# A hybrid decoder layer on one core: x scaled ahead of its turning, and turned by transposes

## The chip, the cores and the metric
The kernel runs on one core of a Trainium2 chip. The metric is the device time in microseconds of one launch. The kernel before took 1552.87 us as the median of three runs (1552.44 to 1555.18).

## What is computed
One layer over 512 tokens and 16 meta tokens in front (528 rows, 2048 features, float32), cut here to what the change touches:

```
h    = concat([meta_tokens, x])                               # 528 x 2048
hn   = h * rsqrt(mean(h * h, axis=-1) + 1e-6) * pre_norm_w    # one factor a token, one a feature
proj = hn @ w_in                                              # 2048 x 8320 columns
# two groups of heads work on proj (RWKV-7 time mixing, differential attention),
# each is multiplied by a SiLU gate
y    = concat([y_r, y_d]) @ w_out
out  = (h + rms_norm(y, post_norm_w))[16:]
```

## The kernel before
The core's five engines each have a program of their own, and semaphores tie them together: SP (SyncE) issues the loads, ScalarE, VectorE and GpSimd (POOL) do elementwise work, TensorE multiplies and turns.

All projections need hn with features on partitions: 16 feature tiles of 128 partitions by 528 tokens. Products are made in three parts to keep float32 precision: each operand is split in a high and a low part (`hn_hi`, `hn_lo`, `w_hi`, `w_lo`), and three products are summed (`feature_tile`, L517). The weights come in units of four 128x128 tiles through a ring of four slots `w_raw`; ScalarE casts the high part (`split_hi`, L843) and POOL makes the low part (`split_lo`, L1086), which frees the slot for SP's next load.

At the start x comes in with tokens on partitions: four tiles `xin[:, t, :]` of 128 x 2048 and the 16 meta rows `xm`. SP loads meta, x tile 0, the constants c32 (they hold the identity), x tiles 1 to 3, ten small parameter rows and then four weight units. The factor of a token goes through three engines, in the order meta, 0, 1, 2, 3: ScalarE squares a tile and sums it (L852), VectorE makes mean + eps (L1150), POOL raises it to -1/2 (L1094). VectorE then multiplies the identity by the factors of each tile (`norm_d`, L1156), copies the turned parameters (`par`, L1159) and makes six small derived ones.

TensorE first turns the parameters (L524), waits for `par_made` and for all five `norm_spread`, and enters the loop that this case is about (L530 to L548). In step k it turns feature tile k by five float32 products, x's tile as the stationary operand and the scaled diagonal as the moving one: 16 meta columns (L535) and four times 128 (L539), into `ma` for even k and `mb` for odd k. From k = 2 on it waits for `hn_lo_made` of k-2, since the PSUM tensor has to be free. ScalarE makes `hn_hi` from it with pre_norm_w as scale (L857), and VectorE `hn_lo` (L1170). From k = 4 on step k also makes the six products L517 of feature tile k-4 for the low-rank tile. ScalarE casts one weight unit in each of the steps 0 to 3.

Behind the loop TensorE goes on with the last four feature tiles and the projections of the first head pair. VectorE sums up the lambda products, clears the padded buffers and signals `zeroed`; then the low-rank tile is finished, and the loops over head pairs follow.

Of the kernel before, what the change touches and what calls it, by code (L numbers as in the profile page):

```python
# [34 lines left out]
P = 128  # L35
D = 2048
# [35 lines left out]
for _name, _rows in (("mu_r", 8), ("mu_k", 8), ("mu_v", 8), ("mu_l", 1), ("w0", 8), ("a0", 8), ("k_k", 8), ("k_a", 8),  # L72
                     ("r_k", 8), ("gn_w", 8), ("gn_b", 8), ("pre", 16), ("sub", 1)):
    PC[_name] = _n
    _n += _rows
N_PAR = _n


# [39 lines left out]
def hybrid_layer(nc, x, meta_tokens, pre_norm_w, w_in, rwkv_mu, rwkv_w0, rwkv_w_up, rwkv_a0, rwkv_a_up,  # L118
# [3 lines left out]
    with ctx:  # L122
# [110 lines left out]
        junk = carve("start", "junk", D)  # L233
        norm_d = carve("start", "norm_d", 5 * P)

# [47 lines left out]
        def s(name):  # L283
            if name not in S:
                S[name] = sem(name)
            return S[name]
# [132 lines left out]
        def _(sp):  # L419
            xs = x[0].rearrange("(t p) d -> p t d", p=P)  # L420
            sp.dma_start(xm[0:META, :], meta_tokens).then_inc(s("meta_in"), 16)
            sp.dma_start(xin[:, 0, :], xs[:, 0, :]).then_inc(s("x_in0"), 16)
            sp.dma_start(c32[:], c32_dram).then_inc(s("const_in"), 16)
            for t in range(1, 4):
                sp.dma_start(xin[:, t, :], xs[:, t, :]).then_inc(s(f"x_in{t}"), 16)
            sp.dma_start(par_rows[0:25, :], rwkv_mu[0].rearrange("(r c) -> r c", c=P)).then_inc(s("par_in"), 16)
# [77 lines left out]
        def _(pe):  # L504
# [21 lines left out]
            pe.wait_ge(s("par_made"), 1)  # L526
            pe.wait_ge(s("norm_spread"), 5)


            for k in range(KT + LORA_LAG):  # L530
                if k < KT:
                    o = (ma, mb)[k % 2]
                    if k >= 2:
                        pe.wait_ge(s("hn_lo_made"), k - 1)
                    mm(o[:, TURN:TURN + META], xm[0:META, k * P:(k + 1) * P], norm_d[0:META, 4 * P:4 * P + META],  # L535
                       start=True, stop=True)
                    for t in range(4):
                        at = TURN + META + t * P
                        last = mm(o[:, at:at + P], xin[:, t, k * P:(k + 1) * P], norm_d[:, t * P:(t + 1) * P],  # L539
                                  start=True, stop=True)  # L540
                    last.then_inc(s("x_turned"), 1)
                if k >= LORA_LAG:
                    h, c = divmod(k - LORA_LAG, UK)
                    pe.wait_ge(s("hn_lo_made"), k - LORA_LAG + 1)
                    pe.wait_ge(s("lo_done"), h + 1)
                    last = feature_tile(tiles[0], h, h, c, True)
                    if c == UK - 1:
                        last.then_inc(s("unit_used"), 1)  # L548
# [286 lines left out]
        def _(act):  # L835
# [9 lines left out]

            for n, t in enumerate((4, 0, 1, 2, 3)):
                act.wait_ge(s(f"x_in{t}" if t < 4 else "meta_in"), 16)
# [233 lines left out]
        def _(pool):  # L1081
# [8 lines left out]
            pool.wait_ge(s("power_made"), 1)  # L1090
            for n, t in enumerate((4, 0, 1, 2, 3)):
                rows = P if t < 4 else META
# [48 lines left out]
        def _(dve):  # L1141
# [4 lines left out]

            for n, t in enumerate((4, 0, 1, 2, 3)):
                rows = P if t < 4 else META
                dve.wait_ge(s("norm_sq"), n + 1)
                TS(norm_s[0:rows, 5 + t:6 + t], norm_s[0:rows, t:t + 1], 1.0 / D, EPS, ALU.mult,  # L1150
                   ALU.add).then_inc(s("norm_var"), 1)
            dve.wait_ge(s("const_in"), 16)
            for n, t in enumerate((4, 0, 1, 2, 3)):
                rows = P if t < 4 else META
                dve.wait_ge(s("norm_pow"), n + 1)
                TS(norm_d[0:rows, t * P:t * P + rows], ident[0:rows, 0:rows], norm_s[0:rows, 10 + t:11 + t], None,  # L1156
                   ALU.mult).then_inc(s("norm_spread"), 1)
            dve.wait_ge(s("par_turned"), 1)
# [316 lines left out]
```

## Time and profile before
| what | value |
|---|---|
| median of the runs | 1552.87 us |
| span of the profiled execution | 1549.4 us |
| PE, PE weight loads busy | 93%, 81% of the span |
| DVE, ACT, POOL busy | 50%, 37%, 31% |
| share of the chain that ended last | PE 76%, DVE 14% |
| mean granted TensorE clock | 0.983 |

The span runs from the first to the last instruction of one profiled execution; of that execution the page gives no other time. PE is TensorE, DVE VectorE, ACT ScalarE. L535 is line 535 of the kernel. The granted clock is given as a share of 2.4 GHz.

### The profile page before, as it was taken

How to read it: one execution, taken by the hardware profiler on the slowest of the kernel's cores; microseconds unless marked ns; L12 is line 12 of the kernel's file. 1: busy time of each engine (PE TensorE's matmuls, PEld its weight loads, DVE VectorE, ACT ScalarE, POOL GpSimd, SP SyncE). 2: the span in 40 equal slices, each digit the busy share in tenths (PEclk: the TensorE clock that was granted, in tenths of full speed). 3: DMA queues.
4: the chain of work that ended last, by engine and by line, in shares of the span. 5: the costliest groups of instructions: out<-in, count | busy, mean ns of one | idle time of the engine just before them, and what ended most of it. 6: DMA issues, size and time to landing. Idle time of an engine off the chain costs nothing.

```text
span 1549.4 us, 26552 instructions
## 1 busy us (share of the span) xinstructions
PE 1436.7 (93%) x9929; PEld 1257.3 (81%) x9929; DVE 767.5 (50%) x1560; ACT 576.3 (37%) x1204; POOL 476.7 (31%) x361
## 2 busy tenths in 40 slices
PE   5998999999999999999999988999999999989994
PEld 4988889788897888988879786978878879768883
DVE  2326566665666666667666544344343443540003
ACT  5332343333434334343333253434444434432321
POOL 2341232222322223232232232334333333324442
PEclk9999999999999999999999999999999999999997
DMA  5221111111111111111111121222222222215322
GB/s 190 71 84 42 42 44 49 50 41 41 42 47 44 43 44 42 47 42 41 47 42 49 50 73 50 70 69 70 69 68 68 61 68 68 68 58 205 117 95 111
DMA packets 151637, 101.43 MB, mean 65 GB/s; under 512 B 6446, under 2 KB 140688, under 8 KB 150416
## 3 DMA queue, kind: packets, MB, share of 16 engines
q1 hardware_dynamic: 151584, 100.71, 21.2%
q8 instruction: 35, 0.57, 0.1%
q14 instruction: 18, 0.15, 0.0%
HBM read 96.49 MB, written 4.19 MB: 65 GB/s over the span
## 4 chain that ended last, share of the span: by engine, by line
PE 76%; DVE 14%; issue 4%; ACT 3%; DMA 1%; POOL 1%; DVEq 0%; SPq 0%; ACTq 0%; POOLq 0%
PE tile L517 39%; PE ma L623 3%; PE tile L784 2%; PE tile L785 2%; PE tile L786 2%; PE ma L644 1%; PE ma L658 1%; DVE arena L1333 1%; PE ma L651 1%; PE mb L709 1%; PE ma L661 1%; DVE arena L1308 1%; PE mb L765 1%; PE ma L786 1%; PE ma L784 1%
## 5 line engine op out<-in xcount | busy, mean ns | idle before, releaser
L1086 POOL TENSOR_TENSOR w_lo<-w_raw,w_hi 128x512 fp32r<-128x512 f32 x324 | 429.3, 1326 | 1012.7 <-ACT w_hi L843 1012.6
L517 PE MATMUL tile<-hn_hi,w_hi 128*128 128x264 f32 (+1 forms) x1696 | 455.5, 331 | 0.0
L517 PE MATMUL tile<-hn_hi,w_lo 128*128 128x264 f32 (+1 forms) x1696 | 436.6, 320 | 0.0
L517 PE MATMUL tile<-hn_lo,w_hi 128*128 128x264 f32 (+1 forms) x1696 | 435.7, 320 | 0.0
L843 ACT CAST w_hi<-w_raw 128x512 fp32r<-128x512 f32 x324 | 200.3, 619 | 425.3 <-PE tile L517 315.1
L517 PEld LDWEIGHTS tile<-hn_hi,w_hi 128*128 128x128 f32 x1696 | 280.0, 190 | 25.6 <-issue 7.2
L517 PEld LDWEIGHTS tile<-hn_hi,w_lo 128*128 128x128 f32 x1696 | 277.6, 190 | 13.3
L517 PEld LDWEIGHTS tile<-hn_lo,w_hi 128*128 128x128 f32 x1696 | 277.3, 190 | 11.0 <-issue 0.5
L1321 DVE TENSOR_TENSOR arena<-ma,c 128x384 f16<-128x384 f32 x120 | 66.7, 556 | 54.7 <-PE ma L644 52.5
L979 ACT ACTIVATE arena<-ma 128x384 f16<-128x384 f32 x120 | 58.5, 487 | 89.0 <-PE ma L658 88.5
L1330 DVE CAST arena<-ma 128x384 f16<-128x384 f32 x120 | 66.6, 555 | 49.3 <-PE ma L661 47.9
L623 PE MATMUL ma<-arena 128*128 128x192 f32 x288 | 59.6, 343 | 12.2 <-issue 12.2
L1405 DVE COPY arena<-mb 128x128 f32<-128x128 f32 x32 | 9.3, 290 | 103.6 <-PE mb L767 103.6
L976 ACT ACTIVATE arena<-ma 128x384 f32<-128x384 f32 x72 | 35.2, 489 | 68.2 <-PE ma L651 68.2
L623 PEld LDWEIGHTS ma<-arena 128*128 128x128 f32 x288 | 47.8, 195 | 15.3 <-issue 13.9
L784 PE MATMUL tile<-w_hi,hn_hi 128*128 128x512 f32 x128 | 53.6, 419 | 5.5 <-DVE hn_lo L1423 5.5
L1308 DVE TENSOR_TENSOR arena<-arena,c 128x384 f16<-128x384 f16 x144 | 52.2, 404 | 0.8
L785 PE MATMUL tile<-w_lo,hn_hi 128*128 128x512 f32 x128 | 51.6, 403 | 0.0
L786 PE MATMUL tile<-w_hi,hn_lo 128*128 128x512 f32 x128 | 51.3, 401 | 0.0
L1101 POOL TENSOR_TENSOR arena<-arena,power 128x4 f32<-128x4 f32 (+2 forms) x25 | 39.1, 1566 | 33.1 <-DVE arena L1409 13.3
L992 ACT ACTIVATE arena<-arena 128x128 f32<-128x128 f32 x72 | 28.8, 400 | 52.7 <-DVE arena L1354 36.5
L658 PE MATMUL ma<-arena 128*128 128x128 f16 x360 | 41.3, 223 | 3.8 <-DVE arena L1321 3.8
(252 smaller groups left out, 2242.5 us busy)
## 6 DMA issues: line engine op xcount, KB each, us to landing
w_raw<-w_in SPq DMA_DIRECT2D x260, 256.0 KB, 2.8
w_raw<-w_out SPq DMA_DIRECT2D x64, 256.0 KB, 2.5
big<-x SPq DMA_DIRECT2D x4, 1024.0 KB, 8.9
arena<-x SPq DMA_DIRECT2D x4, 1024.0 KB, 9.7
out<-big SPq DMA_DIRECT2D x4, 768.0 KB, 3.6
arena<-post_norm_w SPq DMA_DIRECT2D x1, 1024.0 KB, 4.9
out<-big SPq DMA_DIRECT2D x4, 256.0 KB, 2.5
arena<-table_rope SPq DMA_DIRECT2D x2, 264.0 KB, 2.9
```

The source lines that it names most:

```text
L517: last = mm(o[:, at:at + n], w[:, slot, cols], t[:, kt, tok:tok + n], start=(kt == 0 and w is w_hi and t is hn_hi), stop=(kt == KT - 1 and ...
L623: last = mm(ma[:, c * 256:c * 256 + P + CH], pad[:, cs[c], :], apad_r[:, cs[c], :], start=True, stop=True)
L658: last = mm(bank(0, c), bl(xt16, c), bl(z16, c), start=True, stop=True)
L784: mm(banks[t], hn_hi[:, k, y], w_hi[:, k % RING, :], start=(k == 0), stop=False)
L785: mm(banks[t], hn_hi[:, k, y], w_lo[:, k % RING, :], start=False, stop=False)
L786: last = mm(banks[t], hn_lo[:, k, y], w_hi[:, k % RING, :], start=False, stop=(k == KT - 1))
L843: nc.scalar.copy(w_hi[:, slot, :], w_raw[:, slot, :]).then_inc(s("hi_done"), 1)
L979: A(x16, ma[:, 0:W], ACT.Copy).then_inc(s("x_taken"), 1)
L1086: T(w_lo[:, slot, :], w_raw[:, slot, :], w_hi[:, slot, :].bitcast(F32), ALU.subtract).then_inc(s("lo_done"), 1)
L1308: level = lambda l, o: TT(o, g3(ab_hi), level_masks[:, l, :].unsqueeze(1).broadcast_to([P, GC, P]), ALU.mult)
L1321: TT(g3(z16), g3(ma[:, 512:512 + W]), ident16.unsqueeze(1).broadcast_to([P, GC, P]), ALU.add).then_inc(s("zz_taken"), 1)
L1330: V.tensor_copy(xt16, ma[:, 512:512 + W]).then_inc(s("xt_taken"), 1)
```

## The change
The diagonals `norm_d` go. VectorE multiplies each tile of x, and the meta rows, by its tokens' factors in place, over all 2048 columns (`scaled`), and TensorE turns the scaled tiles with `nc.tensor.transpose` and the plain identity. The squares of tiles 1 and 3 are taken on VectorE (`squares_here`), those of meta, 0 and 2 stay on ScalarE. TensorE waits for `x_scaled` of all five, and for the parameters as before. SP loads x's four tiles ahead of the constants.

```diff
-        norm_d = carve("start", "norm_d", 5 * P)
+        junk_d = carve("start", "junk_d", D)
...
-            sp.dma_start(xin[:, 0, :], xs[:, 0, :]).then_inc(s("x_in0"), 16)
+            for t in range(4):
+                sp.dma_start(xin[:, t, :], xs[:, t, :]).then_inc(s(f"x_in{t}"), 16)
             sp.dma_start(c32[:], c32_dram).then_inc(s("const_in"), 16)
-            for t in range(1, 4):
-                sp.dma_start(xin[:, t, :], xs[:, t, :]).then_inc(s(f"x_in{t}"), 16)
...
-            pe.wait_ge(s("norm_spread"), 5)
+            pe.wait_ge(s("x_scaled"), 5)
...
-                    mm(o[:, TURN:TURN + META], xm[0:META, k * P:(k + 1) * P], norm_d[0:META, 4 * P:4 * P + META],
-                       start=True, stop=True)
+                    nc.tensor.transpose(o[:, TURN:TURN + META], xm[0:META, k * P:(k + 1) * P],
+                                        ident[0:META, 0:META])
                     for t in range(4):
                         at = TURN + META + t * P
-                        last = mm(o[:, at:at + P], xin[:, t, k * P:(k + 1) * P], norm_d[:, t * P:(t + 1) * P],
-                                  start=True, stop=True)
+                        last = nc.tensor.transpose(o[:, at:at + P], xin[:, t, k * P:(k + 1) * P], ident)
...
-            for n, t in enumerate((4, 0, 1, 2, 3)):
+            for n, t in enumerate((4, 0, 2)):
                 act.wait_ge(s(f"x_in{t}" if t < 4 else "meta_in"), 16)
...
+            def variance(t):
+                rows = P if t < 4 else META
                 TS(norm_s[0:rows, 5 + t:6 + t], norm_s[0:rows, t:t + 1], 1.0 / D, EPS, ALU.mult,
                    ALU.add).then_inc(s("norm_var"), 1)
+            def squares_here(t):
+                dve.wait_ge(s(f"x_in{t}"), 16)
+                if t == 3:
+                    dve.wait_ge(s("norm_sq_dve"), 1)
+                STT(junk_d, token_rows(t), 1.0, token_rows(t), ALU.mult, ALU.mult,
+                    accum_out=norm_s[:, t:t + 1]).then_inc(s("norm_sq_dve"), 1)
+            def scaled(n, t):
+                rows = P if t < 4 else META
                 dve.wait_ge(s("norm_pow"), n + 1)
-                TS(norm_d[0:rows, t * P:t * P + rows], ident[0:rows, 0:rows], norm_s[0:rows, 10 + t:11 + t], None,
-                   ALU.mult).then_inc(s("norm_spread"), 1)
+                v = token_rows(t)
+                TS(v, v, norm_s[0:rows, 10 + t:11 + t], None, ALU.mult).then_inc(s("x_scaled"), 1)
+            dve.wait_ge(s("norm_sq"), 1)
+            variance(4)
+            dve.wait_ge(s("norm_sq"), 2)
+            variance(0)
+            scaled(0, 4)
+            scaled(1, 0)
+            squares_here(1)
+            dve.wait_ge(s("norm_sq_dve"), 1)
+            variance(1)
+            dve.wait_ge(s("norm_sq"), 3)
+            variance(2)
+            scaled(2, 1)
+            squares_here(3)
+            dve.wait_ge(s("norm_sq_dve"), 2)
+            variance(3)
+            scaled(3, 2)
+            scaled(4, 3)
+            dve.wait_ge(s("const_in"), 16)
             dve.wait_ge(s("par_turned"), 1)
```

## Rows read from the trace of the kernel before
**Rows 1.** Head of the page.
```profile
span 1549.4 us, 26552 instructions
```
**Rows 2.** Chain of waits, first 90 us: start us, us, what.
```profile
15.21 2.01 ACT arena L852 x2
...
17.33 1.07 DVE arena L1156 x5
...
18.62 0.60 PE ma L535 x2
...
26.86 1.09 PE ma L539 x8
27.95 0.72 PE tile L517 x6
28.67 0.32 PE mb L535 x2
28.99 1.09 PE mb L539 x8
30.08 0.73 PE tile L517 x6
...
51.48 38.53 PE tile L517 x315
```
**Rows 3.** Turning: groups by shape (count, busy us, mean ns), and timeline near 108 us.
```profile
L539 PE MATMUL ma<-arena,big 128*128 128x128 f32 x64 | 10.2, 307 | 0.0
L597 PE MATMUL mb<-c,arena 128*128 128x128 f32 x40 | 5.9, 279 | 1.0
108.19 0.74 PE L597 MATMUL mb<-c,arena 128*128 128x128 f32 x5
```
**Rows 4.** Timeline, 19 to 28 us: start us, us, instruction.
```profile
19.16 2.08 PE L539 MATMUL ma<-arena,big 128*128 128x128 f32 x8
...
25.38 1.16 PE L539 MATMUL mb<-arena,big 128*128 128x128 f32 x8
...
26.57 0.70 ACT L857 ACTIVATE hn_hi<-mb,par 128x528 fp32r<-128x528 f32 x1 [0.46 <-PE mb L539]
...
27.17 0.61 ACT L843 CAST w_hi<-w_raw 128x512 fp32r<-128x512 f32 x1
27.31 0.77 DVE L1170 SCALAR_TENSOR_TENSOR hn_lo<-mb,par,hn_hi 128x528 fp32r<-128x528 f32 x1 [0.90 <-ACT hn_hi L857]
```
**Rows 5.** Timeline, 52 to 55 us.
```profile
52.94 0.21 DVE L1175 TENSOR_TENSOR arena<-arena 128x64 f32<-128x64 f32 x1
53.00 1.30 POOL L1086 TENSOR_TENSOR w_lo<-w_raw,w_hi 128x512 fp32r<-128x512 f32 x1 [1.06 <-ACT w_hi L843]
...
53.44 0.94 DVE L1175 TENSOR_TENSOR arena<-arena 128x64 f32<-128x64 f32 x1
```
**Rows 6.** VectorE's groups by shape: count, busy us, mean ns, idle before.
```profile
L1374 DVE TENSOR_TENSOR arena<-arena 128x512 f32<-128x512 f32 x8 | 11.0, 1375 | 0.7 <-ACT arena L880 0.7
...
L1267 DVE SCALAR_TENSOR_TENSOR arena<-arena 128x576 f32<-128x576 f32 x8 | 6.0, 751 | 0.0
...
L1372 DVE TENSOR_TENSOR arena<-xk,arena 128x512 f32<-128x512 f32 x8 | 5.5, 685 | 0.0
...
L1400 DVE TENSOR_SCALAR arena<-arena 128x528 f32<-128x528 f32 x8 | 4.0, 496 | 0.3
...
L1400 DVE TENSOR_SCALAR arena<-arena 128x144 f32<-128x144 f32 x8 | 2.4, 295 | 0.3
```
**Rows 7.** Timeline of the start.
```profile
8.91 0.57 POOL L1094 TENSOR_TENSOR arena<-arena,power 128x1 f32<-128x1 f32 x1 [2.51 <-DVE arena L1150]
10.03 1.91 ACT L852 ACTIVATE arena<-big 128x2048 f32<-128x2048 f32 x1 [1.39 <-DMA big<-x]
...
16.54 0.40 PE L524 MATMUL ma<-c,arena 98*128 98x98 f32 x1 [16.54 <-DMA arena<-diff_subln_w]
```
**Rows 8.** Windows: stretch, length, busy us of PE, PEld, DVE, ACT, POOL, granted clock, DMA.
```profile
120.00:125.00 5.00, 4.87 (x17) 4.90 (x18) 2.06 (x5) 0.00 (x0) 0.00 (x0) 0.50 0.00 0
125.00:130.00 5.00, 4.57 (x40) 4.14 (x40) 2.74 (x7) 2.14 (x5) 1.28 (x1) 0.96 0.04 10
...
900.00:904.00 4.00, 2.24 (x19) 2.03 (x17) 3.90 (x6) 2.40 (x5) 1.31 (x1) 1.00 0.24 68
```

More of the change, by code:

```diff
@@ L76 @@
 N_PAR = _n
+NORM_ORDER = (4, 0, 1, 2, 3)
 def constants():
@@ L1090, in _ @@
             pool.wait_ge(s("power_made"), 1)
-            for n, t in enumerate((4, 0, 1, 2, 3)):
+            for n, t in enumerate(NORM_ORDER):
                 rows = P if t < 4 else META
@@ L1144, in _, with token_rows @@
             TT, STT, TS = V.tensor_tensor, V.scalar_tensor_tensor, V.tensor_scalar
-            for n, t in enumerate((4, 0, 1, 2, 3)):
+            def token_rows(t):
+                return xin[:, t, :] if t < 4 else xm[0:META, :]
+            def variance(t):
                 rows = P if t < 4 else META
-                dve.wait_ge(s("norm_sq"), n + 1)
                 TS(norm_s[0:rows, 5 + t:6 + t], norm_s[0:rows, t:t + 1], 1.0 / D, EPS, ALU.mult,
                    ALU.add).then_inc(s("norm_var"), 1)
-            dve.wait_ge(s("const_in"), 16)
-            for n, t in enumerate((4, 0, 1, 2, 3)):
+            def squares_here(t):
[5 more added lines that the diff above has]
+            def scaled(n, t):
                 rows = P if t < 4 else META
                 dve.wait_ge(s("norm_pow"), n + 1)
-                TS(norm_d[0:rows, t * P:t * P + rows], ident[0:rows, 0:rows], norm_s[0:rows, 10 + t:11 + t], None,
-                   ALU.mult).then_inc(s("norm_spread"), 1)
+                v = token_rows(t)
[18 more added lines that the diff above has]
+            dve.wait_ge(s("const_in"), 16)
             dve.wait_ge(s("par_turned"), 1)
```

## The prediction
> **What bounds the kernel now.** I read the page's header first: the span is 1549.4 us [rows 1]. It is 3.5 us under the median of the runs, 1552.87, and the page gives no other time for that execution. I work on the span and carry the difference over to the median. Next I read the chain of waits over the first 90 us [rows 2]. It has three parts. Until 18.6 us no product of the layer runs: the chain goes over the loads of x, two squares on ScalarE and five small VectorE multiplications, and TensorE starts at 18.62. From there to 51.5 us the chain never leaves TensorE for long: it alternates between turning one feature tile of x (L535 for the 16 meta rows, L539 for the other 512) and the six low-rank products of an earlier tile (L517). From 51.5 it stays in L517 for 38.53 us. So a microsecond off the turning loop is a microsecond for everything behind it, and a microsecond of later start costs one.
>
> The turning is matrix products with a scaled diagonal. The view by shapes shows 64 records at L539 for each of the two PSUM tensors, 128 for 16 x 4 = 64 products: two records for each f32 product [rows 3]. The turns that the kernel makes elsewhere as real transposes have 40 records at L597 for 8 x 5 transposes, one each [rows 3]. Five of them lie in 0.74 us, of which the last takes 0.27: (0.74 - 0.27) / 4 = 0.12 us apart [rows 3]. In the loop one L539 record costs 1.09 / 8 = 0.136 us on the chain [rows 2].
>
> **The change part by part.** (1) *Turning by transposes.* A turn now costs 0.32 + 1.09 = 1.41 us [rows 2] and has ten records; it keeps five. Half is 0.70; with 0.12 apart it would be 0.6. I take 0.70, because the meta piece and the change of PSUM bank keep their edges. A step of the loop is then 0.70 + 0.73 (six L517) = 1.43 instead of 2.14 us. Is another engine next? ScalarE needs 0.70 for hn_hi, VectorE 0.77 for hn_lo [rows 4], and turn k+2 has to wait for hn_lo of k: 0.70 + 0.70 + 0.77 + about 0.12 of handing over = 2.3 us per two steps, against 2.86 on TensorE. So TensorE still sets the pace, with 0.28 us a step to spare. From turn 5 to turn 15 there are eleven such turns: 11 x 0.71 = **7.8 us gained**.
>
> (2) *The first five turns.* TensorE is slow there: the first eight records take 2.08 us, 0.25 each, those from 25.38 on 1.16 us, 0.14 each [rows 4]. The granted clock in the profile says 1.00 for this stretch too, so I go by the spacing: the lower of the two levels, 1.2 GHz, until some 4.8 us after the first product. Before, turn 4 ends and the first L517 starts 27.95 - 18.62 = 9.33 us after TensorE's start [rows 2]. After, with T as the start, turns 0 and 1 end at T+1.27 and T+2.54. hn_lo of 0 is ready at T+2.8, so turn 2 runs to T+4.1. ScalarE has a weight cast of 0.61 us [rows 4] between its hn_hi, so hn_lo of 1 is ready at T+4.1 and turn 3 ends at T+5.4. hn_lo of 2 comes at T+5.6, and turn 4 (at full clock by then) ends at T+6.4. **2.9 us gained**, not the 4.6 that the halved records would give, since here the hn_hi-hn_lo loop is next. POOL's first w_lo (1.30 us each [rows 5]) is ready at about T+4 and isn't late.
>
> (3) *The start.* The five diagonal multiplications (1.07 us [rows 2]) and two of ScalarE's squares go; VectorE gets two squares over 2048 columns and five scalings over 2048 in place, all in one queue, and TensorE waits for the last. Durations: the scaling by a pointer scalar, in place, in SBUF (L1400), takes 295 ns for 144 columns and 496 for 528 [rows 6]: 0.52 ns a column, for 2048 columns 496 + 1520 x 0.52 = 1.29 us. That row is the same operation in the same place, so it decides; the upper bound is one column in 1.03 ns as below, 2.27 us. The square is a two-input operation: 685 ns for 512 and 751 for 576 columns [rows 6], 1.03 ns each, so 751 + 1472 x 1.03 = 2.27 us; upper bound by L1374, 1375 ns for 512, twice that. Reading the accumulator is taken as 0.15. Nothing excludes a little less than any of these, by 0.1 each.
>
> Now the queue. VectorE is free at 8.85, when POOL takes the power for x's first tile [rows 7]; the meta power is long done. Two scalings: 11.4. Square of tile 1, which landed before 10.03 even in the old order [rows 7]: 13.85. Two variances: 14.15. POOL's power, 0.57 with handing over 0.65 [rows 7]: 14.8. Scaling of 1: 16.1. Square of 3: 18.5. Variance 18.7. Scalings of 2 and 3: 21.3. Copy of the parameters, the 0.22 us between 18.40 and 18.62 in the chain [rows 2]: 21.6. There is a second effect. VectorE's two-input operation of 64 columns took 0.21 us alone and 0.94 beside POOL's w_lo, ending with it [rows 5]. POOL's powers of 0.57 fall beside VectorE's new long operations three times, so each may wait for the other: 0 to 1.7 us. I take 0.5: T = 22.1, **3.5 us lost** against 18.62. Bounds: 21.0 to 23.3 with the durations above, 33 with both upper bounds.
>
> (4) *Order of the loads.* x's tiles 1 to 3 go ahead of the 368 KB of constants in SP's queue; ten small parameter loads stay behind both. The bytes in front of the parameters are the same, so their turn at 16.54 [rows 7] stays, far ahead of the new T. Tile 3 may come 0.9 us earlier; VectorE reaches it at 16.1, so it is worth nothing: VectorE hides it. Nothing else on SP moves. The constants aren't needed before that 16.54. The loss if this cover fails is at most about 1 us.
>
> (5) *What lies behind.* The rest of the start on VectorE (lambda, clearing, the signal that lets ScalarE finish the low-rank tile) is counted from hn_lo of tile 15, the weight loads from POOL's w_lo: all move with the loop. TensorE never waits between 51.5 and 90 us [rows 2], so I let the whole shift through to the end.
>
> Sum: + 3.5 - 2.9 - 7.8 = -7.2 us. 1552.87 - 7.2 = **1545.6 us**.
>
> **Rivals.** *A late clock.* What raises the clock might be products, and not transposes. Then the low level lasts past the first products: turn 4 costs 1.27, and a step costs 1.27 + 2 x 0.73 = 2.7 us until the clock rises. If it rises 4.8 us after the first L517 as it did after the first product, two steps and a half run slow: 2.5 x 1.3 = 3.2 us. Time: 1548.8. For it: the four turns before the first L517 will hold no product at all, and no row shows the clock rise on transposes alone. Against: nothing in the trace tells the two apart. The Trainium skill, "TensorE: Matmul & The Clock Gate", Part 4, states just this, that the full clock doesn't engage in transpose mode since that mode isn't taken for a busy engine in the same way; by that rule the sum is this rival's. No run here shows it yet.
>
> *The clock stays low through the loop* (slower than before). In the loop half of TensorE's time would be transposes. If the clock stayed at its lower level, 1.2 GHz, with that mix, eleven steps would cost 2.73 instead of the old 2.14 us, + 6.5; the first five turns end at T+7 instead of 9.33, - 2.3; the start + 3.5: +7.7 us, 1560.6. It decides from the point where the low level outlasts about eight steps. Against it: between 900 and 904 us TensorE is busy 2.24 of 4 us and the granted clock stays at 1.00; between 120 and 125 us, behind an idle stretch, it is 0.50, and in the next five us it is up at 0.96 [rows 8].
>
> *VectorE's start is longer than its price.* If scaling runs at one column in 1.03 ns and the squares at L1374's rate, T moves by 4 x 0.98 + 2 x 2.27 = 8.5 us: 1554.1. With the scaling alone, 1549.5. For it: L1374 is such an operation at double price [rows 6]. Against: its twin of the same size takes 685 ns, and the rows at double price lie in stretches where POOL makes w_lo, which the start hasn't got.
>
> *The gain is swallowed.* A wait behind 51.5 us that isn't counted from the loop would keep its date: about no change, 1552.9. I see none in the chain.
>
> **How the numbers follow.** Forecast 0.50 (1543 to 1547.5); late clock 0.27; longer start 0.10; swallowed 0.07; low clock 0.06. A measurement of this kernel tells about 0.2%, 3.1 us, from no change, so faster means under 1549.8. Faster: 0.50 + 0.24 of the late clock + 0.03 of the longer start = 0.77. Same: 0.03 + 0.04 + 0.07 = 0.14. Slower: 0.03 + 0.06 = 0.09. The range, 1542.5 to 1551.0, starts where T is 21.0 and a transpose costs 0.12 us throughout with a microsecond for the runs' spread, and ends a little above the late clock and the slower scaling.
>
> **What would show each step right or wrong.** One record for each transpose at the new turning line, 0.12 to 0.14 us apart; TensorE's first transpose of x at 21.0 to 23.3 us; VectorE's scalings at 1.2 to 1.4 us and its squares at 2.2 to 2.5; steps of 1.43 us in the chain with TensorE at its head; the end of turn 15 at about 44.3 instead of 51.48. The forecast is wrong if records stay 0.25 us apart beyond the first L517, if the turn's cost isn't halved, or if the later stages don't keep their distance to the end of the loop.

## The result and the profile after
The changed kernel takes 1572.93 us (five runs, 1569.84 to 1588.62) against 1553.17 of the kernel before: ratio 1.0144, interval 1.0103 to 1.0184. It is slower by some 20 us where 7 us of gain were forecast. The profiled run is the longest of the five, 1588.62 us; its span is 1586.6 us where that of before is 1549.4 [rows 1]. Every ratio in this document is against the kernel before, measured in the same series.

```profile
span 1586.6 us, 26391 instructions
...
q8 instruction: 79, 1.29, 0.3%
```

The second row is from the page's list of DMA queues (packets, MB, share of the span): q8 is a queue that carries instructions, 16 KB a packet. The kernel before has 35 packets and 0.57 MB there.

First the part that the change touches. The chain of waits of the changed kernel, first 90 us:

```profile
21.08 0.28 PE ma L534
...
26.99 0.28 PE ma L534
27.27 1.04 PE ma L538 x4
28.31 1.32 PE tile L517 x6
...
33.33 0.73 PE tile L517 x6
34.07 0.16 PE mb L534
34.23 0.59 PE mb L538 x4
...
46.65 43.54 PE tile L517 x338
```

A turn has half its records, as forecast (x4 for x8 of [rows 2]), and at full clock a step costs 0.16 + 0.59 + 0.73 = 1.48 us instead of 2.14. TensorE starts 2.5 us later. But the fifth turn and the first six L517 still cost 1.32 us each: at 28.3 us the clock is at its lower level, where it was up by 25.4 us before [rows 4]. (The granted clock in the profile says 1.00 all through the start, so here, as in the prediction, the level is read from the pace of the records.) Turn 15 ends at 46.65 instead of 51.48, 4.8 us earlier. Up to here the change is a gain.

The profiled run's span is 37.2 us longer all the same, so it loses 42 us later. In the waits of TensorE over the whole span (engine, line, waited for: us in total, times, longest) one row has nothing to answer it in the kernel before:

```profile
PE tile L517 <- POOL w_lo L1084: 15.4, 5, 3.3
PE ma L750 <- DVE arena L1411: 15.3, 5, 3.1
```

The second row, L752 before, was there with the same 15.3. The first is new: five stops. The releaser is only inferred, and the timeline shows that it isn't the one:

```profile
287.08 0.40 PE L517 MATMUL tile<-hn_hi,w_lo 128*128 128x512 f32 x1
...
288.73 1.26 POOL L1084 TENSOR_TENSOR w_lo<-w_raw,w_hi 128x512 fp32r<-128x512 f32 x1 [3.58 <-ACT w_hi L841]
290.81 0.50 PEld L517 LDWEIGHTS tile<-hn_hi,w_hi 128*128 128x128 f32 x2 [3.77 <-POOL w_lo L1084]
```

287.48 is the end of one pass of the loop over head pairs, and 290.81 the first product of the next. The w_lo at 288.73 is that of a unit three ahead, and it ends at 289.99, before TensorE goes on. In the kernel before the same place, with the same w_lo at 294.55, has no gap: its last product of a pass starts at 292.92 and the next at 293.15.

```profile
292.92 0.40 PE L517 MATMUL tile<-hn_hi,w_lo 128*128 128x512 f32 x1
293.15 0.41 PE L517 MATMUL tile<-hn_hi,w_hi 128*128 128x264 f32 x2
```

What follows the stop, in windows of the changed kernel (columns as in [rows 8]):

```profile
287.50:290.80 3.30, 0.00 (x0) 0.00 (x0) 0.69 (x1) 1.81 (x3) 1.26 (x1) 0.74 0.05 13
290.80:297.00 6.20, 6.19 (x27) 5.11 (x28) 0.20 (x2) 0.70 (x1) 0.00 (x0) 0.59 0.02 5
```

The granted clock behind the stop is 0.59, where it is 1.00 in the undisturbed stretches: it falls to the lower level during the stop and TensorE works at it for about 5 us. Behind the second stop (390.87 to 393.63) the low level lasts some 10 us (granted clock 0.51 from 394.6 to 404.8), and so it does at the other three. So a stop costs its own length and half of the low stretch again. The first product of the stage that follows (L582 before, L580 after) comes once a pass. From the weight load of the first one to that of the last, seven passes on, the kernel before takes 780.9 - 101.9 = 679.0 us and the changed one 814.6 - 97.1 = 717.5: 38.5 us for five turns of the loop. Of these 15.4 are the stops. Between 95 and 820 us the granted clock, read in windows of 5 us, gives 51 us at the lower level against 7 before. Half of the 44 more is 22 us, and with the stops that is nearly all of it. The mean granted clock of this run is 0.966, that of the other four is 0.976 to 0.978; over the span that is some 16 us of time (an estimate), as much as the profiled run is longer than the median.

And between 300 and 790 us the instruction queue moves one packet before and forty after (first row before, second after):

```profile
q8 instruction: 1, 0.02, 0.0%
```
```profile
q8 instruction: 40, 0.66, 0.6%
```

So instructions are loaded anew in each pass of the loop, and TensorE stands still at its turn. That the loading is what stops it is only argued so far, and the question became why it should happen, since the change touches no line of the loop.

### The profile page after: what moved, and what is told of

Its sections match the earlier page's. It is cut to its first block, busy times and chain, and to the rows that moved or that the text cites. A ratio compares the mean times of both kernels' runs of the same rounds, so it can differ in the third digit from the quotient of the medians.

```text
span 1586.6 us, 26391 instructions
## 1 busy us (share of the span) xinstructions
PE 1453.3 (92%) x9849; PEld 1264.6 (80%) x9849; DVE 777.2 (49%) x1564; ACT 573.1 (36%) x1200; POOL 479.6 (30%) x361
## 3 DMA queue, kind: packets, MB, share of 16 engines
q8 instruction: 79, 1.29, 0.3%
## 4 chain that ended last, share of the span: by engine, by line
PE 75%; DVE 15%; issue 5%; ACT 3%; POOL 1%; DMA 0%; DVEq 0%; ACTq 0%; SPq 0%; POOLq 0%
PE tile L517 39%; PE ma L621 3%; PE tile L782 2%; PE tile L783 2%; PE tile L784 2%; PE ma L642 1%; PE ma L656 1%; DVE arena L1362 1%; PE ma L649 1%; PE mb L707 1%; PE ma L659 1%; DVE arena L1337 1%; PE mb L763 1%; PE ma L784 1%; PE mb L708 1%
## 5 line engine op out<-in xcount | busy, mean ns | idle before, releaser
L517 PE MATMUL tile<-hn_hi,w_hi 128*128 128x264 f32 (+1 forms) x1696 | 461.4, 335 | 15.4 <-POOL w_lo L1084 15.4
L517 PE MATMUL tile<-hn_hi,w_lo 128*128 128x264 f32 (+1 forms) x1696 | 440.6, 323 | 0.0
L517 PE MATMUL tile<-hn_lo,w_hi 128*128 128x264 f32 (+1 forms) x1696 | 439.8, 323 | 0.0
L517 PEld LDWEIGHTS tile<-hn_hi,w_hi 128*128 128x128 f32 x1696 | 284.2, 193 | 43.0 <-POOL w_lo L1084 17.5
L517 PEld LDWEIGHTS tile<-hn_hi,w_lo 128*128 128x128 f32 x1696 | 281.0, 192 | 13.6
L517 PEld LDWEIGHTS tile<-hn_lo,w_hi 128*128 128x128 f32 x1696 | 281.5, 193 | 11.1 <-issue 0.5
```

Source lines behind the costliest of these rows:

```text
L517: last = mm(o[:, at:at + n], w[:, slot, cols], t[:, kt, tok:tok + n], start=(kt == 0 and w is w_hi and t is hn_hi), stop=(kt == KT - 1 and ...
```

## The experiments
**What was counted.** In the built program a float32 product is four instructions of TensorE (two weight loads, two products), any other product and a transpose two, a wait by itself one. The loop over RWKV head pairs (`Fori(2, 8)`) is 1598 instructions; the traces of both kernels have as many of TensorE's records in a pass (754 products and 844 weight loads). It starts 2637 instructions into TensorE's program in the kernel before and, since 80 products became transposes, 160 earlier, 2477, in the changed one. The Trainium skill, "Runtime: NRT & Kernel Launch", section Instruction fetch mechanics, says that instructions come in 16 KiB blocks of 256, that TensorE's instruction memory has room for 2048, and that a taken branch to a target outside the current window, which it gives as two pages, stops the engine for a fetch. 1.29 MB in 79 packets, 16.3 KB each, agrees with the block. The window of two pages doesn't agree: 1598 instructions are more than six blocks, and in the kernel before the turn of the loop fetches nothing (one packet in 490 us). By the block alone 1598 instructions lie in seven blocks, or in eight when the loop starts in the last 61 places of one.

**Only the loop's place: padding.** 160 waits on a long-landed load, ahead of everything that TensorE does, bring the loop back to 2637.

```diff
+            for _ in range(320):          # two of them make one instruction
+                pe.wait_ge(s("meta_in"), 16)
             pe.wait_ge(s("const_in"), 16)
             pe.wait_ge(s("par_in"), 16 * 10)
```

> The changed kernel with 160 instructions more on TensorE ahead of everything it does (waits for the meta rows, which have long landed), so that its first loop over head pairs stands 2637 instructions into TensorE's program as in the kernel before, and not 2477. Theory A (place of the loop): the 3.3 us that TensorE stands still at each turn of that loop, and the low clock behind them, come from where the loop stands in the program; they go, the instruction queue q8 falls from 79 packets to about 35, and what is left is the turning's own gain seen in the profile, the end of turn 15 at 46.65 instead of 51.48: about 1549 us (1547 to 1551). Theory B (time): the loops run into the low clock because everything comes 5 us earlier; padding changes nothing: 1570 to 1589 us, 79 packets. Theory C (other engines): VectorE's and ScalarE's longer and shorter programs do it: 1570 to 1589 us.

Measured: 1549.82 us (ten runs, 1545.34 to 1551.24), ratio 0.9972, interval 0.9958 to 0.9986; q8 is back at 35 packets, the stops are gone. A change of place alone takes back 23 us. The 160 waits aren't free: they end at 20.95 us and hold back the turning of the parameters, so the first turn comes at 21.77 instead of 21.08 us.

**The kernel before, moved.** The same with 96 waits in the kernel before: the loop at 2733.

```diff
+            for _ in range(192):
+                pe.wait_ge(s("meta_in"), 16)
```

> The kernel before, nothing of the change, with 96 such waits more on TensorE: its first loop stands 2733 instructions into the program, which leaves the same remainder by 256 (173) as the changed kernel's 2477. Theory A: it gets slow like the changed kernel, with a stop of about 3.3 us at each turn of the loop and q8 at about 79 packets: 1553 + about 24 = 1577 us (1572 to 1590). Theories B and C: 1553 us, 35 packets.

Measured: 1579.49 us, ratio 1.0161, interval 1.0138 to 1.0183. One of its runs took 6491.86 us, and one of the fourteen of the kernel before in the same series 1883.5 us; nothing here explains either, and neither is part of the ratio. The other three lie between 1575.83 and 1580.9. Its page and its waits of TensorE:

```profile
q8 instruction: 80, 1.31, 0.3%
```
```profile
PE tile L517 <- POOL w_lo L1088: 14.3, 5, 3.0
```

The five stops appear in a kernel that has nothing of the change. Behind four of them the clock is low for 3.4 us, with one for 13.7. That theories B (time) and C (the other engines' programs) fall, this run alone shows: no other engine's program was touched, and the padding lies in TensorE's first wait.

**A third place.** 64 waits in the changed kernel: the loop at 2541.

> The changed kernel with only 64 such waits: the loop stands at 2541, a remainder of 237 by 256, neither the old nor the changed one. Theory A in its sharp form: the loop's 1598 instructions lie in seven blocks of 256 or in eight, and only a start in the last 61 places of a block makes it eight. The changed kernel is in that stretch, so 64 places on it must be out of it: about 1549 us and 35 packets. A weaker form of A (the stretch of bad places is wider than 61): 1570 us or more. Theories B and C: 1570 to 1589 us.

Measured: 1545.54 us (1545.23 to 1547.71), ratio 0.9962, interval 0.9948 to 0.9977, 35 packets. This is the change as it is without the accident of its place: 7.3 us faster than before, and 27.4 us faster than the changed kernel. The stops and the clock account for that too: 15.4 us of stops, and a mean granted clock of 0.976 in the changed kernel's median run against 0.983 here, which over the span is some 23 us more at the lower level and costs half of them (an estimate, 27 us in all). The end of turn 15 is at 45.74 us.

**Two more places, 62 apart.** 31 waits in the changed kernel (2508, remainder 204) and 65 in the kernel before (2702, remainder 142), one run each.

> The changed kernel with 31 waits more: the loop at 2508, remainder 204 by 256. The bad stretch of places is, by seven or eight blocks of 256 for 1598 instructions, 61 long and holds the remainder 173, but not 77 and 237. So of the remainders 204 and 142 (the next run), which lie 62 apart, one at most can be slow. Slow is 79 packets on q8 and 1570 us or more, fast is 35 packets and 1544 to 1551 us. If both are slow, the stretch is wider than this reckoning, and something else than the loop's own blocks counts too.

> The kernel before with 65 waits more: the loop at 2702, remainder 142 by 256. As said at the run with remainder 204: not both slow. Slow is about 80 packets on q8 and 1576 us or more, fast is 35 packets and 1551 to 1556 us.

Measured: 1550.77 us and 34 packets for the first, 1578.13 us and 80 packets for the second. With the others, by remainder:

| kernel | place | remainder by 256 | q8 packets | us |
|---|---|---|---|---|
| before | 2637 | 77 | 35 | 1552.9 |
| before, 65 waits | 2702 | 142 | 80 | 1578.1 |
| before, 96 waits | 2733 | 173 | 80 | 1579.5 |
| changed | 2477 | 173 | 79 | 1572.9 |
| changed, 31 waits | 2508 | 204 | 34 | 1550.8 |
| changed, 64 waits | 2541 | 237 | 35 | 1545.5 |
| changed, 160 waits | 2637 | 77 | 35 | 1549.8 |

All five remainders go as a bad stretch of 61 places would have it, if that stretch covers 142 and 173, and the kernels further below, all at 2637, 2541 or 2540, are fast too. Its last places by the count would be the remainders 195 to 255; 204 and 237 are fast, so the blocks' edges don't lie where a count from the program's first instruction puts them, and the exact ends weren't measured. Why eight blocks aren't kept where 2048 instructions would be eight blocks stays open; that one more is fetched ahead would do it, and the 44 or 45 packets more for five turns are nine a turn and not eight, but no run was made to show it.

**The transposes alone undone.** x still scaled in place, but turned by float32 products with the identity, the meta rows too. The loop is at 2637 without padding.

```diff
-                        last = nc.tensor.transpose(o[:, at:at + P], xin[:, t, k * P:(k + 1) * P], ident)
+                        last = mm(o[:, at:at + P], xin[:, t, k * P:(k + 1) * P], ident, start=True, stop=True)
```

> The changed kernel with the turning alone undone: x is still scaled in place on VectorE, but turned by f32 products with the identity. That has the 160 instructions that the transposes saved, so the loop over head pairs stands at 2637 as in the kernel before, without padding. It separates the transposes from the rest. Theory A (place) with the start's price: TensorE starts at 21.1 instead of 18.6 us, the loop of turns takes as long as in the kernel before (32.9 us), turn 15 ends at 53.9 instead of 51.48: 1552.9 + 2.5 = 1555.4 us (1553.5 to 1557), 35 packets on q8, and the clock rises within some 5 us of TensorE's start since there are products from the start. Rival (the scaled x or the order of loads slows the later stages): 1570 us or more.

Measured: 1556.58 us (twelve runs, 1551.3 to 1558.42), ratio 1.0016, interval 1.0006 to 1.0026, 35 packets. The end of its loop:

```profile
55.70 0.32 PE mb L534 x2
56.02 1.09 PE mb L538 x8
57.11 2.93 PE tile L517 x24
```

The late start without the transposes, with a late clock (see below), is a loss of 0.16%, some 2.5 us; the transposes are worth 11.0 us (1556.58 to 1545.54). The end of turn 15 is at 57.1, not at the 53.9 that I expected, because here too the clock rises late: four turns take 2.08 us for eight records and the fifth 1.74, where the kernel before has 1.16 from the third on. Is that the run's doing, the kernel's, or that of the second operand's values (the identity, where before it was a diagonal)? Three single runs: the same kernel once more, the kernel before once more, neither with an edit, and the first with the centring matrix (the identity less 1/64 inside each 64x64 block) in the place of the identity, which leaves out the layer's right values and counts for its time alone:

```diff
-                        last = mm(o[:, at:at + P], xin[:, t, k * P:(k + 1) * P], ident, start=True, stop=True)
+                        last = mm(o[:, at:at + P], xin[:, t, k * P:(k + 1) * P], c32v("centre"), start=True, stop=True)
```

> The kernel with float32 products for transposes once more, unchanged. In its first look eight records took 2.00 us until 31.9 us, 12 us behind TensorE's start. If the moment of the rise is a property of the run, it comes elsewhere now, between 4 and 12 us behind the start; if it is the kernel's, at about 33 us again. 1551 to 1558 us.

> The kernel before once more, unchanged. In the profile of before the clock rose at about 23 us, 4.5 us behind TensorE's start; in the two moved copies at about 25 and 27 us. If the moment is the run's, it comes elsewhere now; if the kernel's, at 23. 1550 to 1555 us.

> As after_products, but the 128-column products of the turning take the centring matrix of the constants (identity less 1/64 inside each 64x64 block) instead of the identity, so that hn holds other values than the layer's: only its time counts. It has the same instructions and places, and 64 nonzero values a column instead of one. If the rise depends on the values, it comes within 5 us of TensorE's start (by 26 us); if not, it scatters as in the others, up to 12 us behind the start.

Measured: 1558.74, 1547.39 and 1558.67 us. The second lies 2.6 us below the range I gave and below every other run of the kernel before (from 1550.04 us), so single runs of one kernel tell little about a few microseconds. Three turns of the first in TensorE's timeline: the fourth and fifth are slow, the sixth, the first behind an L517, is at full pace:

```profile
29.38 2.08 PE L538 MATMUL mb<-c,big 128*128 128x128 f32 x8
...
31.92 2.00 PE L538 MATMUL ma<-c,big 128*128 128x128 f32 x8
...
34.90 1.16 PE L538 MATMUL mb<-c,big 128*128 128x128 f32 x8
```

The centring matrix has the same times within 0.1 us, and the kernel before has its third turn at 1.16 us again, at 23.01, and ends turn 15 at 50.78. So the moment of the rise came again in each kernel that was repeated, and the operand's values don't set it. With products and hardly a gap it came some 4 to 5 us after TensorE's first turn in the kernel before and some 12 us after it in the kernel with products. The two moved copies of the kernel before, with the same turns, lie between: their third turn still takes 1.99 us (65 waits) and 1.68 (96 waits), and the fourth is the first at 1.16, so the clock rose some 7 us after the first turn. One difference between the two kernels is the idle time of TensorE ahead of the first turn, 4.2 to 4.3 us against 1.0 and 1.7; but the moved copies have 1.0 and 1.8 and are late as well, so that idle time alone doesn't set the moment. What does stays open.

**The order of the loads undone**, at place 2541.

```diff
-            for t in range(4):
-                sp.dma_start(xin[:, t, :], xs[:, t, :]).then_inc(s(f"x_in{t}"), 16)
-            sp.dma_start(c32[:], c32_dram).then_inc(s("const_in"), 16)
+            sp.dma_start(xin[:, 0, :], xs[:, 0, :]).then_inc(s("x_in0"), 16)
+            sp.dma_start(c32[:], c32_dram).then_inc(s("const_in"), 16)
+            for t in range(1, 4):
+                sp.dma_start(xin[:, t, :], xs[:, t, :]).then_inc(s(f"x_in{t}"), 16)
```

> The changed kernel at the good place 2541, with the order of loads of the kernel before (the constants between x's tiles 0 and 1). My reckoning: VectorE and not the loads sets the start, so nothing moves: TensorE starts at 21.1, 1545.5 us (within 1.5). Rival: the order is worth up to 0.9 us at the start, since x's tile 0 landed at 6.06 instead of 6.64 in the changed kernel: up to 0.6 us more, 1546.1, which shows in the profile as a later start of VectorE's scalings (8.7 instead of 8.16 us).

Measured: 1547.40 us (1545.08 to 1550.16), ratio 0.9960, interval 0.9947 to 0.9972. TensorE's first turn comes at 21.23 instead of 21.05 us. ScalarE gets tile 2 a microsecond later (12.07 for 11.00), and VectorE, busy with its own square until 13.5, waits 0.4 us at most. The medians are 1.9 us apart and their intervals overlap, so no worth of the order can be told; at TensorE's first turn it is 0.2 us.

**All squares on ScalarE**, at place 2541, with VectorE's first scaling held until POOL has its second power.

```diff
-            for n, t in enumerate((4, 0, 2)):
+            for n, t in enumerate(NORM_ORDER):
...
             dve.wait_ge(s("norm_sq"), 2)
             variance(0)
+            dve.wait_ge(s("norm_pow"), 2)
             scaled(0, 4)
             scaled(1, 0)
-            squares_here(1)
...
+            for n, t in ((2, 1), (3, 2), (4, 3)):
+                dve.wait_ge(s("norm_sq"), n + 1)
+                variance(t)
+                scaled(n, t)
```

> The changed kernel at the good place 2541, with all five squares on ScalarE; VectorE only scales, and starts once POOL has its second power, so that no scaling lies beside the first two. If VectorE's queue sets the start (two squares of 2.28 us, and three powers held up to 1.53 us beside its scalings), TensorE's first turn comes at about 18.3 instead of 21.1 us, and the time falls by 2.5 to 2.8 us against the padded kernel: 1542.9. If the loads or ScalarE set it, it stays at 20 us or later: 1544.5 to 1546.

Measured: 1546.77 us (1542.3 to 1549.3), ratio 0.9950, interval 0.9934 to 0.9965. Its chain:

```profile
2.62 11.07 DMA big<-x
13.71 2.01 ACT arena L852 x2
...
18.07 0.29 PE ma L536
```

The start does what I expected of it, 18.07 instead of 21.05 us, and turn 15 ends at 43.31 instead of 45.74. The medians don't follow: the six runs are two at 1542.3 and 1542.6 and four from 1546.7 on. The mean granted clock tells them apart: 0.983 in the two, 0.978 to 0.980 in the four, so these have more time at the lower level later in the span. Three runs of the padded kernel have 0.983 too, and they took 1545.2 to 1545.5 us. At the same clock the earlier start is thus worth 2.9 us; in the medians, where later stretches of low clock come in that differ from run to run, it doesn't show.

**Holding the clock up with products.** First eight products of the identity with itself into an unused PSUM tile, where TensorE waits for x, with 128 waits (place 2637):

```diff
                                 ).then_inc(s("par_turned"), 1)
+            for _ in range(8):
+                mm(tiles[1][:, 0:P], ident, ident, start=True, stop=True)
             pe.wait_ge(s("par_made"), 1)
```

> The changed kernel with the loop's place as in the kernel before (128 waits and 32 instructions of eight added f32 products of the identity with itself, into an unused PSUM tile). The products run from about 16.9 us on, while TensorE waits for the scaled x until 21.1, and cost nothing by themselves. If products raise TensorE's clock and transposes don't (late clock), the transposes of x are 0.12 to 0.15 us apart from about 21.7 us on instead of 0.28, unless the stretch of transposes alone lets the clock fall again; the first L517 come at 0.12 apart, and the time is 3 to 5 us under the same kernel without the products, about 1545. If transposes raise the clock as products do, the products bring the rise forward as well and the two can't be told apart by this run alone; if the clock falls again in the transposes, the time is that of the padded kernel, 1549.

Measured: 1545.11 us (1542.44 to 1545.5), ratio 0.9951, interval 0.9932 to 0.9969; at the same place without the products it was 1549.82. TensorE in its timeline:

```profile
17.94 3.67 PE L529 MATMUL tile<-c 128*128 128x128 f32 x16
...
21.76 1.11 PE L542 MATMUL ma<-c,big 128*128 128x128 f32 x4
...
24.69 0.66 PE L542 MATMUL ma<-c,big 128*128 128x128 f32 x4
...
25.80 0.66 PE L542 MATMUL mb<-c,big 128*128 128x128 f32 x4
...
27.15 1.11 PE L542 MATMUL ma<-c,big 128*128 128x128 f32 x4
27.92 0.79 PE L517 MATMUL tile<-hn_hi,w_hi 128*128 128x264 f32 x2
...
31.49 0.66 PE L542 MATMUL ma<-c,big 128*128 128x128 f32 x4
```

The same four transposes take 1.11, then 0.66, then 1.11 and again 0.66 us: up behind the products, down behind four turns of transposes with idle gaps between them, up again behind the L517. Whether the transposes or the gaps let it fall, this run can't tell. Then two products more behind each of the first four turns, no padding needed (place 2541):

```diff
                     last.then_inc(s("x_turned"), 1)
+                    for _ in range(2 if k < LORA_LAG else 0):
+                        mm(tiles[1][:, 0:P], ident, ident, start=True, stop=True)
```

> The changed kernel with 16 added f32 products of the identity with itself: eight while TensorE waits for the scaled x, and two behind each of the first four turns, where it waits for hn_lo. 64 instructions, so the loop is at 2541. In the run with eight products ahead alone, the third turn ran at full pace and the fifth at the low one again. If products raise and hold the clock and transposes do neither, all turns from the third on are at 0.15 us a record and the first L517 at 0.12: the fifth turn and the first L517 cost 0.74 and 0.73 us instead of 1.33 and 1.32, and the time is 1.5 to 2.5 us under 1545.1, about 1543. If transposes had nothing to do with it, the clock would fall at the fifth turn as before: 1545.

Measured: 1542.82 us (1541.73 to 1546.34), ratio 0.9937, interval 0.9925 to 0.9949. Its chain has no slow turn at all:

```profile
21.18 0.23 PE ma L538
21.41 0.58 PE ma L542 x4
21.99 0.45 PE tile L545 x4
...
26.29 0.59 PE ma L542 x4
26.88 0.72 PE tile L517 x6
```

Turn 15 ends at 43.13, 2.6 us ahead of the padded kernel's 45.74.

**The same places filled with transposes.** Each of the 16 added products, two records and two weight loads, is replaced by two transposes of the identity. The instruction count, the place 2541 and the filled gaps stay; only the kind of work changes.

```diff
-            for _ in range(8):
-                mm(tiles[1][:, 0:P], ident, ident, start=True, stop=True)
+            for _ in range(16):
+                nc.tensor.transpose(tiles[1][:, 0:P], ident, ident)
...
-                    for _ in range(2 if k < LORA_LAG else 0):
-                        mm(tiles[1][:, 0:P], ident, ident, start=True, stop=True)
+                    for _ in range(4 if k < LORA_LAG else 0):
+                        nc.tensor.transpose(tiles[1][:, 0:P], ident, ident)
```

> The run with 16 added products (clock up through all turns, 1542.8 us) with 32 transposes of the identity in their place: the same 64 instructions, the same places in TensorE's queue, loop at 2541. If transposes raise and hold the clock as products do, it is up by the first turn (0.58 us for four transposes of x at 21.4 us) and the time is 1543. If they do neither, the turns and the first L517 run slow (1.06 and 1.32 us) until some microseconds behind the first L517, and the added transposes, 0.13 to 0.25 us each at the low clock, even delay the first four turns by up to 1 us each where these don't wait: 1546 to 1549 us.

Measured: 1544.74 us (four runs, 1541.84 to 1546.05), ratio 0.9941, interval 0.9924 to 0.9957. TensorE in its timeline; L545 and L529 are the added transposes:

```profile
16.70 3.62 PE L529 MATMUL tile<-c 128*128 128x128 f32 x16
...
21.31 1.12 PE L542 MATMUL ma<-c,big 128*128 128x128 f32 x4
22.22 1.06 PE L545 MATMUL tile<-c 128*128 128x128 f32 x4
...
23.43 1.11 PE L542 MATMUL mb<-c,big 128*128 128x128 f32 x4
24.34 0.74 PE L545 MATMUL tile<-c 128*128 128x128 f32 x4
...
25.17 0.66 PE L542 MATMUL ma<-c,big 128*128 128x128 f32 x4
...
27.99 0.49 PE L517 MATMUL tile<-hn_hi,w_hi 128*128 128x264 f32 x2
```

From the parameters' turn at 16.5 us up to the L517 at 27.99 TensorE runs nothing but transposes, and idles once for 0.78 us. The pace rises at about 24.5 us all the same and stays up: in every turn from 25.17 on the four transposes take 0.66 us. Here transposes almost without gaps raised the clock and held it, later than products in the same places (24.5 against no later than 21.2). The end of turn 15, 44.48, lies between the 43.13 of the products and the 45.74 of the padded kernel.

**Both together**: squares on ScalarE and 16 added products (four each around the turning of the parameters, two behind each of four turns), place 2540.

> Two findings put together, at the good place 2540: all five squares on ScalarE (TensorE's first turn at 18.07 instead of 21.05 us) and 16 added products of the identity that hold TensorE's clock up through the turns (four before and four behind the turning of the parameters, two behind each of the first four turns). Against the run with the products alone, whose turn 15 ended at 43.13 us, I expect the end of turn 15 at about 40.3, and 2.8 us less in all: 1540.0 (1538 to 1543, since the stretches of low clock later on come in steps of 3.4 us). If the clock has not risen by the first turn (only eight products from some 14.5 us on), the turns start slow and about 1 us of it is lost.

Measured: 1541.57 us (1541.35 to 1545.24), ratio 0.9932, interval 0.9919 to 0.9946. TensorE's first turn is at 18.73, its first four transposes still take 0.96 us, and turn 15 ends at 41.05 where I expected 40.3 (the total lies within the 1538 to 1543 that I gave). It is the fastest version, 11.5 us under the kernel before of the same runs and 31 under the changed kernel.

## Why the prediction was wrong
*The step that failed* is part 5, "all move with the loop" and "I let the whole shift through to the end", in which the length of the program stood at nothing without a reason. The shift at the end of turn 15 did go through; beside it the change took 160 instructions out of TensorE's program, and with them moved a loop that it doesn't touch. That costs 27.4 us in the medians (1572.93 against 1545.54), and 38.5 us between the first and the last pass in the profiled run. None of the rivals had it. I had weighed the halved records as time and never as length of program.

*The sum.* + 3.5 - 2.9 - 7.8 = -7.2 us; the changed kernel at a good place has -7.3 in the medians, but this agreement is luck. In the padded kernel's profile (64 waits) the start costs 2.4 us (21.05 for 18.62), the first five turns gain 2.1 (7.2 us for 9.33) and the steps from there to the end of turn 15 gain 6.1 (17.45 for 23.53): -5.7 in all, and in the other profiles turn 15 ended at 46.4 to 47.0 instead of the forecast 44.3. The rest of the agreement lies within the 4 to 8 us by which runs of one such kernel differ.

*Part 1*, the turn at half price: right. 0.75 us at full clock for a forecast 0.70; with 0.73 for the products a step is 1.48 for 1.43.

*Part 2 and the late clock.* The forecast had the clock up 4.8 us after TensorE's start. In the changed kernel it rose by about 32.5 us, 11 us after it, behind the first L517 at 28. That is the rival "late clock": turn 4 and up to two steps slow (in the padded kernel it rose in the second step, by 31 us). The times are the rival's; its reason, that transposes don't raise the clock, falls with the run whose gaps were filled with them. The Trainium skill, "TensorE: Matmul & The Clock Gate", Part 4, states that the full clock doesn't engage in transpose mode. By that rule the clock of that run would have stayed low until the first L517 at 27.99, and it was up at 24.5, so here the measurement decides against it. What failed in my step is the figure of 4.8 us, taken from one kernel: with products throughout it was 4 to 5 us in one kernel, 7 in its two moved copies and 12 in another. Shown is that work added on TensorE, while it waits for x and for hn_lo, brings the rise forward, products more than transposes. What sets the moment otherwise stays open.

*Part 3*, the start: T = 21.08 for a forecast 22.1 (21.0 to 23.3). The prices were right: scaling 1.27 to 1.29 us for 1.29, square 2.28 for 2.27, the accumulator 0.08 for 0.15. Two of POOL's powers took 1.53 instead of 0.57 us, as feared, and VectorE waited 0.47 and 0.44 us for them, where 0.5 was allowed in all. The difference the other way is x's tile 0, ready at 6.06 instead of 6.64 (6.20 in the run with the old order of loads, so most of it isn't the order's doing), and about 0.1 us of overlap between neighbouring VectorE instructions, which I had added up. One slip doesn't touch the forecast: the rival with the longer start counts four scalings where the queue has five, and by its own prices should say 1555.1 instead of 1554.1.

```profile
8.16 1.27 DVE L1167 TENSOR_SCALAR arena<-arena 16x2048 f32<-16x2048 f32 x1
8.33 1.53 POOL L1092 TENSOR_TENSOR arena<-arena,power 128x1 f32<-128x1 f32 x1 [1.83 <-DVE arena L1151]
9.89 1.29 DVE L1167 TENSOR_SCALAR big<-big,arena 128x2048 f32<-128x2048 f32 x1 [0.47 <-POOL arena L1092]
11.03 1.91 ACT L850 ACTIVATE arena<-big 128x2048 f32<-128x2048 f32 x1 [2.96 <-DMA big<-x]
11.10 2.28 DVE L1159 SCALAR_TENSOR_TENSOR arena<-big 128x2048 f32<-128x2048 f32 x1
```

POOL's power begins beside VectorE's scaling and ends behind it (9.86); the next scaling needs it. ScalarE stood idle 2.96 us before its last square: the work that was moved to VectorE had a free engine where it was, and left there it brings TensorE's first turn to 18.07 us.

*Part 4*, the order of loads: right, worth nothing that can be told.

## What to carry to other kernels
A change of TensorE's instruction count ahead of a loop moves the loop in the program, and a long loop body (1598 instructions here) can then be loaded anew in each pass: count the instructions, look at the instruction queue's packets inside the loop, and before judging a change, run it padded to the old place. A stop at the turn of a loop that the waits put down to an engine long done is the sign of it. Don't carry the moment of the clock's rise from one kernel to another that starts differently; here a few products in the gaps of a sparse start brought it up and kept it up, at no cost that shows, since TensorE waited there anyway. Work moved to balance two engines has to be laid along the chain first: here the "free" engine's queue was the chain.

## What was not expected of the hardware
- The same stretch with the loop costs 679 us or, with the loop at a bad place, 705 to 718 us in the profiled runs (before, and its copies with 65 and 96 waits, and the changed kernel): 35 or 79 to 80 packets of instructions, five stops of 2.6 to 3.4 us, and with all but one of them the clock at 1.2 GHz for 3 to 14 us.
- The clock fell during turns of transposes with gaps between them (full pace at 25.80, lower level at 27.15), and didn't fall again where more transposes filled the gaps.
- With products all along and hardly a gap, the clock rose 4 to 5 us after the first turn in the kernel before (two profiled runs), some 7 us after it in its two moved copies, and some 12 us after it in the kernel with products for transposes (three).
- POOL's 128x1 power takes 0.57 us alone and 1.53 beside a VectorE scaling of 1.28 us over 2048 columns: it finishes behind it. A ScalarE square beside a VectorE square isn't held up (1.91 us from 11.03 on, as in the kernel before).
- One run of the moved kernel before took 6491.86 us and one of the kernel before 1883.5 us, both in one series; nothing like it came back.
